# A fourth slot for split weights, norms moved into units, and a new order of work at a gate, in a two-block transformer kernel on one Trainium2 core

## The reference

```python
def _layer(x, ...):                                  # the first block
    h = _rmsnorm(x, ln1_g)
    q, k, v, u = jnp.split(h @ w_in, [...], axis=-1) # 1024, 256, 256, 1024 wide
    q = _rmsnorm(q.reshape(bsz, L, 16, 64), q_norm_g)
    k = _rmsnorm(k.reshape(bsz, L, 4, 64), k_norm_g)
    y_attn = _sliding_window_attention(q, k, v, attn_sinks, rel_bias)   # window 128
    y_ssm = _s5_mixer(u, ..., w_glu)                 # scan over time; y * sigmoid(y @ w_glu)
    mixed = jnp.concatenate([_rmsnorm(y_attn, attn_out_g), _rmsnorm(y_ssm, ssm_out_g)], axis=-1)
    x = x + mixed @ w_out
    h2 = _rmsnorm(x, ln2_g)
    return x + (jax.nn.silu(h2 @ w_ff_gate) * (h2 @ w_ff_up)) @ w_ff_down   # hidden 5632

def second_block(x, ...):                            # two layers
    for layer in range(2):
        hn = rmsnorm(h, norm_mix_pre[layer])
        mix = gmlp_shortconv_mixer(hn, ...) if layer % 2 == 0 else dilated_attention_mixer(hn, ...)
        h = h + rmsnorm(mix, norm_mix_post[layer])
        f = squared_relu_mlp(rmsnorm(h, norm_mlp_pre[layer]), w_up[layer], w_down[layer])  # 8192
        h = h + rmsnorm(f, norm_mlp_post[layer])

def gmlp_shortconv_mixer(h, w_in, w_s, b_s, conv_w, w_out):
    a_u, a_v, g_b, g_c, b_x = jnp.split(h @ w_in, [...], axis=-1)
    a_u, vf = jax.nn.gelu(a_u), jax.nn.gelu(a_v)
    mu = jnp.mean(vf, axis=-1, keepdims=True)
    var = jnp.mean(jnp.square(vf - mu), axis=-1, keepdims=True)
    vn = (vf - mu) * lax.rsqrt(var + LN_EPS)         # v's norm
    mixed = einsum('gts,bnsgc->bntgc', where(causal, w_s, 0), vn) + b_s
    z = g_c * b_x                                    # then a causal convolution of width 3
    return concatenate([a_u * mixed, g_b * y]) @ w_out

def dilated_attention_mixer(h, w_qkv, w_o, positions):
    q, k, v = jnp.split(h @ w_qkv, 3, axis=-1)       # 16 heads of 128, rope on q and k
    ...                                              # three dilations, joined by a softmax
```

## Time and profile before

| | |
|---|---|
| median of 3 runs | 3328.59 us (3328.2 to 3331.68) |
| the profiled execution, its own time | 3326.39 us |
| its span in the trace | 3324.4 us |
| mean granted TensorE clock | 0.989 of full speed |
| busy PE / PEld | 3237.1 us (97%) / 2671.3 (80%) |
| busy DVE / ACT / POOL | 1866.3 us (56%) / 1472.2 (44%) / 80.8 (2%) |
| idle of PE | 3324.4 - 3237.1 = 87.3 us |
| DMA | 593 MB, mean 178 GB/s, 55% of the 16 engines' time |

### The profile page before, as it was taken

How to read it: one execution, slowest core, us unless ns; L and a number is a source line. 1 busy time by engine, 2 the same in 40 slices (tenths; PEclk the granted TensorE clock), 3 DMA queues, 4 the chain that set the end, 5 groups by cost and what they waited for, 6 DMA issues and landing times. The chain is left out here.

```text
span 3324.4 us, 38815 instructions
## 1 busy us (share of the span) xinstructions
PE 3237.1 (97%) x15938; PEld 2671.3 (80%) x15938; DVE 1866.3 (56%) x1978; ACT 1472.2 (44%) x1757; POOL 80.8 (2%) x76
## 2 busy tenths in 40 slices
PE   8989999999999999999999999999999999999998
PEld 6877888888888778878888888878877788888886
DVE  7655655554555545665555555665655655555555
ACT  6534544444444444444444444444444544444443
POOL 1120000000000000000000000000000000000000
PEclk9999999999999999999999999999999999999999
DMA  6334555555555555555555555545455555555554
GB/s 207 113 112 116 177 184 189 191 192 193 193 188 192 179 172 189 192 177 188 189 188 192 189 191 189 189 159 178 151 165 165 176 190 188 189 188 188 187 189 150
DMA packets 185517, 593.19 MB, mean 178 GB/s; under 512 B 12491, under 2 KB 17276, under 8 KB 184828
## 3 DMA queue, kind: packets, MB, share of 16 engines
q1 hardware_dynamic: 185340, 590.70, 54.7%
HBM read 588.54 MB, written 2.12 MB: 178 GB/s over the span
## 5 line engine op out<-in xcount | busy, mean ns | idle before, releaser
L1155 DVE TENSOR_TENSOR LO<-RAW,HI 128x1024 fp32r<-128x1024 f32 (+1 forms) x1104 | 1346.3, 1222 | 1133.4 <-ACT HI L593 1131.2
L593 ACT ACTIVATE HI<-RAW 128x1024 fp32r<-128x1024 f32 (+1 forms) x1104 | 1158.9, 1052 | 1352.4 <-PE PS L2054 1344.0
L2054 PE MATMUL PS<-HI,KPA 128*128 128x512 f32 x5312 | 1476.6, 394 | 13.5 <-ACT HI L593 5.5
L2054 PEld LDWEIGHTS PS<-HI,KPA 128*128 128x128 f32 x5312 | 992.9, 189 | 224.3 <-issue 12.2
L2054 PE MATMUL PS<-HI,KPB 128*128 128x512 f32 x3392 | 935.2, 392 | 4.0 <-DVE ACC L1757 3.4
L2054 PE MATMUL PS<-LO,KPA 128*128 128x512 f32 x2656 | 828.6, 392 | 5.8 <-DVE LO L1155 5.8
L2054 PEld LDWEIGHTS PS<-HI,KPB 128*128 128x128 f32 x3392 | 631.0, 188 | 133.1 <-issue 5.3
L2054 PEld LDWEIGHTS PS<-LO,KPA 128*128 128x128 f32 x2656 | 501.0, 189 | 115.7 <-DVE LO L1155 8.7
L2054 PE MATMUL PS<-LO,KPB 128*128 128x512 f32 x1696 | 524.5, 390 | 0.8 <-DVE KPB L1193 0.8
L2054 PEld LDWEIGHTS PS<-LO,KPB 128*128 128x128 f32 x1696 | 318.6, 188 | 68.8 <-issue 1.2
L622 ACT ACTIVATE KPB<-PS 128x512 fp32r<-128x512 f32 x98 | 58.6, 599 | 181.6 <-PE PS L2114 181.6
(11 more groups left out here) (268 smaller groups left out, 1038.2 us busy)
## 6 DMA issues: line engine op xcount, KB each, us to landing
RAW<-in_w_up SPq DMA_DIRECT2D x128, 1024.0 KB, 5.0
RAW<-in_w_down SPq DMA_DIRECT2D x128, 1024.0 KB, 5.4
RAW<-in_w_qkv SPq DMA_DIRECT2D x48, 1024.0 KB, 5.2
RAW<-in_w_ff_gate SPq DMA_DIRECT2D x88, 512.0 KB, 3.8
RAW<-in_w_ff_up SPq DMA_DIRECT2D x88, 512.0 KB, 4.7
RAW<-in_w_ff_down SPq DMA_DIRECT2D x44, 1024.0 KB, 5.4
RAW<-in_w_in_ab SPq DMA_DIRECT2D x40, 1024.0 KB, 5.0
RAW<-in_w_in SPq DMA_DIRECT2D x16, 1024.0 KB, 5.3
```

The source lines that it names most:

```text
L593: e.activation(HI[:, s % NSPLIT, 0:w], RAW[:, d % NRAW, j, 0:w], ACT.Copy).then_inc(S("hi_made"), 1)
L1155: e.tensor_tensor(LO[:, h, 0:w], RAW[:, d % NRAW, j, 0:w], HI[:, h, 0:w].bitcast(F32), ALU.subtract).then_inc(S("lo_made"), 1)
L2054: ins = e.matmul(PS[:, b + j, 0:cw], l, r[:, h, 512 * j:512 * j + cw], start=(i == 0 and part == 0), stop=(last and part == 2))
```

## The change

It has five parts.

1. **A fourth slot.** From the unit ws0 on there is a slot 3 (HI3, LO3) where the state space's tables (CC) lay, from up1.0 on it is slot 4 (HI4, LO4) where small tables of the first block lay. `make_slots` gives every step the slot that was used longest ago (`plan.slot`, and `plan.was`, the step that used it before); `split_by(i)` says how far HI and LO may be made when step i is at hand. Step s is split once the step `was[s]` is done, so now up to four steps back instead of three.
2. **A split between evacuations.** At the end of the six qkv units named in `SPLIT_BETWEEN` the evacuating engine makes its next HI (ACT) or LO (DVE) after tile 0 and before tile 1.
3. **k's norm goes to the q unit, q's norm is denser, y is fed earlier.** The KD multiplications are in `k_norm`, k's root is taken in the q unit. Both squares of q follow each other on ACT (the second into LG1), there are two roots of 16 columns instead of one of 32, and glu's steps ask for y's chunks by the table `Y_DUE`. k's turns follow glu's steps 1 and 2, q's the steps 5 and 6. ACT makes a sigmoid of one element (WARM) before the gate, and at the gate DVE takes the first two logits between the gate's multiplications.
4. **v's norm goes into ab1.** `v_squares` on ACT, centring, mask and scaling in `mixing` on DVE, and TensorE's mixing starts three steps later.
5. **pre0's turns** in dn1.5.1 are taken between the tiles and after the steps (`first_half`, in `mids` and `sides`), instead of only after them.

```diff
+    def make_slots(self):
+        fourth, moved = self.by_name["ws0"].first, self.by_name["up1.0"].first
+        used = {i: i - NSPLIT for i in range(NSPLIT)}
+        self.slot, self.was, self.taken = [], [], {}
+        for s in range(len(self.steps)):
+            if s == fourth:
+                used[3] = s - 1
+            h = min(used, key=used.get)
+            self.slot.append(4 if h == 3 and s >= moved else h)
+            self.was.append(used[h])
+            used[h] = s
...
+    def split_by(self, i):
+        s = i
+        while s + 1 < len(self.steps) and self.was[s + 1] < i:
+            s += 1
+        return s
...
+Y_DUE = (1, 2, 2, 3, 3, 4, 4, 4)
+SPLIT_BETWEEN = ("qkv0.0", "qkv0.1", "qkv0.2", "qkv1.0", "qkv1.1", "qkv1.2")
+def first_half(feeder):
+    yield
+    for _ in range(4):
+        next(feeder)
+        yield
...
-                if s >= NSPLIT:
-                    q.wait_ge(S("step_done"), s - NSPLIT + 1)
-                e.activation(HI[:, s % NSPLIT, 0:w], RAW[:, d % NRAW, j, 0:w], ACT.Copy).then_inc(S("hi_made"), 1)
+                if plan.was[s] >= 0:
+                    q.wait_ge(S("step_done"), plan.was[s] + 1)
+                if s in plan.taken:
+                    taken(plan.taken[s])
+                e.activation(HI[plan.slot[s]][:, 0:w], RAW[:, d % NRAW, j, 0:w], ACT.Copy).then_inc(S("hi_made"), 1)
...
                 evac(0, u.bank[0])
                 q.wait_ge(S("step_done"), u.last + 1)
+                if name in SPLIT_BETWEEN:
+                    hi(plan.split_by(u.last + 1))
                 evac(1, u.bank[1])
...
             for c in range(4):
                 out_of(2 + c, qT, 2 * c, "qg")
+                if c == 3:
+                    e.activation(WARM[:, 0:1], ONE[:, 0:1], ACT.Sigmoid)
...
-        att = late(attn1(), 4)
-        unit("glu", y_feed(), [S0, S1, q_norm(), att], ahead=1)
+        att = late(attn1(), 1)
+        unit("glu", y_feed(), [S0, S1, q_norm(), att], ahead=Y_DUE)
...
-            q.wait_ge(S("v_centred"), t + 1)
-            q.wait_ge(S("v_squared"), t)
-            e.activation(JK[:, :], AV[:, t, :], ACT.Square, accum_out=vs2[:, t:t + 1]).then_inc(S("v_squared"), 1)
+
+        def v_squares():
+            yield
+            for t in range(2):
+                q.wait_ge(S("v_centred"), t + 1)
+                q.wait_ge(S("v_squared"), t)
+                e.activation(JK[:, :], AV[:, t, :], ACT.Square, accum_out=vs2[:, t:t + 1]).then_inc(S("v_squared"), 1)
+                yield
...
-        unit("ab1", None, (), (), to_sb(lambda t: GC[:, t, :], "pre0"))
+        unit("ab1", None, [v_squares()], (), to_sb(lambda t: GC[:, t, :], "pre0"))
...
         for n in range(2):
             gate_times(n)
+        next(att)
         q.wait_ge(S("gated"), 1)
         next(sf)
         for n in range(2, 4):
             gate_times(n)
-        for _ in range(2):
-            next(att)
+        next(att)
...
-        unit("ab1", None, [late(mxg, 3)])
+        unit("ab1", None, [mxg])
...
-                    pend = [part0()] if i == nu // 2 and c == 0 else []
+                    pend = [first_half(nf0[0])] if i == nu // 2 and c == 0 else []
```

More of the change, by code:

```diff
@@ L23 @@
 NSPLIT = 3
-LA = NSPLIT - 1
 SCRATCH = 1024
@@ L286, in in_units @@
     for i in range(n):
-        while feeder is not None and made < due(i, n, ahead):
+        while feeder is not None and made < (ahead[i] if isinstance(ahead, tuple) else due(i, n, ahead)):
             next(feeder)
@@ L760, in ssm @@
             for k in range(4):
-                for _ in range(3):
+                for _ in range(2 if k == 3 else 3):
                     yield
@@ L980, in scalar @@
                 for c in range(2):
-                    unit(f"dn1.{i}.{c}", None, pend)
+                    unit(f"dn1.{i}.{c}", None, pend, mids=pend if i == nu // 2 else ())
                     for g in pend:
                         drain(g)
-                    pend = [part(nf)] if i == nu // 2 and c == 0 else []
+                    pend = [first_half(nf)] if i == nu // 2 and c == 0 else []
         def dn_added(c, t):
@@ L1667, in vector @@
                 for c in range(2):
-                    unit(f"dn1.{i}.{c}", None, pend, (), add_x(c))
+                    unit(f"dn1.{i}.{c}", None, pend, (), add_x(c), mids=pend if i == nu // 2 else ())
                     added(f"dn1.{i}.{c}")
@@ L2006, in gpsimd, with k_root @@
         S0, S1 = ssm(0), ssm(1)
-        unit("q", [S0, S1])
-        root("k")
+        def k_root():
+            for _ in range(11):
+                yield
+            root("k")
+            yield
+        unit("q", [S0, S1, k_root()])
         def q_root():
-            for _ in range(4):
+            for t in range(2):
+                root(f"q{t}")
                 yield
-            root("q")
-            yield
         unit("glu", [S0, S1, q_root()])
@@ L2028, in matmuls @@
             s = u.first + i
-            h, g = s % NSPLIT, G[u.group]
+            h, g = plan.slot[s], G[u.group]
             kt, ks = chunk(g, i)
@@ L2238, in ssm @@
                 yield
-                for i in range(2):
+                for i in range(2 if k < 3 else 1):
                     if k < 3:
@@ L2363, in tensor @@
         unit("q", None, [pr2, S0, S1])
-        att = late(attn1(), 4)
-        unit("glu", None, [S0, S1, att], ahead=1)
-        for _ in range(2):
-            next(att)
+        att = late(attn1(), 1)
+        unit("glu", None, [S0, S1, att])
+        next(att)
         unit("ws0", None, [s_sums(), att], mids=[att])
@@ L2473, in tensor @@
         mxg = mixing()
-        unit("ab1", None, [late(mxg, 3)])
+        mxl = late(mxg, 6)
+        unit("ab1", None, [mxl])
         unit("ab2")
```

145 lines of the change are left out of this document (91 added, 54 removed).

## The result

The changed kernel took 3317.79 us (median of 9 runs, 3315.93 to 3322.01), the kernel before 3328.59 (9 runs, 3324.01 to 3331.68): ratio 0.997, 95% interval 0.9961 to 0.9979, or 10.8 us less where 17.6 were forecast. TensorE's busy time is the same 3237.1 us; its idle time fell from 87.3 to 78.6.

What follows compares the result with a forecast made beforehand. TensorE, busy nearly throughout, was taken as the bound, so only its waits and clock drops could give time. 9.9 + 2.2 + 1.4 + 10.4 - 6.3 = 17.6 us less: 3308.8 profiled, 3311.0 median; range 3302 to 3320.

Steps and rivals of the forecast that it cites:

- signs of being wrong: Waits over 2 us left in glu, new LO waits in ab1, over 10 us more low clock in qkv, or ends not lengthened.
- Glu: Glu unit: three waits for y's chunks go, 8.14, plus 3.4 of clock, less 1.6 for new waits; gain 9.9 us.
- The gate: At the gate: table load, qT copy and DVE's wait for scores come off, one LO is added; gain 2.2 us.
- The fourth slot: End of ws0: takes 1.4 of a 2.13 us wait through an earlier bias transfer; 0 over the other steps.
- The second block's start: Before the second block and around v's norm: waits of 2.65, 1.87, 1.71 go, plus clock 1.7 and 2.5; gain 10.4 us.
- The splits between: Ends of the qkv units: tile 1's bank comes later, 5.35 us, plus 1.0 for the clock; loss 6.3 us.
- the 1.0 for the clock: Qkv ends: a wait of about 3.7 us may drop the clock, costing 1.7 with six chances in ten.
- A: Rival: waits move from glu to the attention, whose DVE work is unchanged; 3319.5 us, chance 0.17.
- parts 1 to 3: The prediction's terms for glu with the q and k norms, the gate, and the fourth slot; 13.5 us together.
- B: Rival: the qkv ends cost only 0.7 and the slot removes small waits, say 2; 3303.4 us, chance 0.17.
- C: Rival: all six qkv ends wait for a late HI and drop the clock, 3.0 + 3.4 each; 3342.7 us, chance 0.03.
- D: Rival: glu's chunks stay late because of the scan, and v's norm makes splits late inside ab1; 3324 us, chance 0.10.

## Why the prediction was right, and where its sizes were off

The direction held, the sum was 6.8 us too good, and the time lies within the stated range. Of the mechanisms, those of glu's new wait, the gate, pre0's turns and the splits between held; the fourth slot's did not, and in two places the gain came from another part of the change than the one I named (k's multiplications, v's norm). In the traces, where the kernels are 8.7 apart, the misses are 0.4 ahead of glu, 1.3 in it, 0.2 at the gate, 2.4 for the slot, 0.6 up to qkv0.0 and 4.6 at the ends, less 0.6 too little at the second block's start. Two of my own signs of being wrong came true: a wait of over 2 us in glu (2.72, for the scan and not for a chunk), and over 10 us more at 1.2 GHz in the qkv units (13.6 against 3.4). By its own steps:

- *Glu.* 8.6 of 9.9. The allowance for new waits was 1.6, and 2.72 came. The chain was named rightly (the last quarter of the second half, GpSimd and DVE), but I took its durations as unshortened and did not see that they would grow: q's multiplication now lies beside GpSimd's last operation, 1.58 instead of 0.73. The roots of 16 columns took 3.42 and 2.91, against 2.9 (GpSimd, the changed kernel, from 198.95 and 205.45 on). That k's multiplication made the chunk late, which I argued from its 2.55 us, was wrong as a cause: with it gone and the old table the 3.31 became 3.73. What made the chunk late was when it was asked for.
- *The gate.* 2.0 of 2.2 in the trace. Undoing the order alone loses 1.9 in the trace and 1.6 in the times, though of what I had counted (table load, qT copy, DVE's wait) no run undoes one by itself. That the table load is off the path is read from the trace only (ACT, the changed kernel; glu ends at 232.49):

```profile
230.58 1.28 ACT L863 ACT_TABLE_LOAD   x1
231.88 0.20 ACT L863 ACTIVATE WARM<-ONE 128x1 f32<-128x1 f32 x1
231.99 1.04 ACT L646 ACTIVATE HI<-RAW 128x1024 fp32r<-128x1024 f32 x1
232.93 1.55 ACT L959 ACTIVATE GT<-PS 128x512 f32<-128x512 f32 x3
```

  The gate's sigmoid starts 0.44 us after glu's end. The sigmoid of one element starts 0.02 after the load's end, so again no drain is to be seen between the load and what follows.
- *The fourth slot.* Forecast 1.4, measured a loss, 1.0 up to the first FFN unit's second chunk. The wait of 2.33 for the bias rows did go: DVE waits 0.71 there for scores now (285.79). But its next logits wait 1.30 for scores, and DVE comes later to the addition that frees the bank: from TensorE's last turns to that addition pass 1.98 us (290.95 and 292.93), before it was 1.53 (302.16 and 303.69). The wait became 2.58, with 3.4 us at 1.2 GHz in every trace with four slots. In the kernel as changed the slot costs 4.1 us (3.4 by the gains), without the splits between 1.8 by the medians and 4.1 by the gains; only with v's norm in its old place does it take something away, 5.4 us of wait and clock. That it removes nothing over the other steps was right: ACT's HI's wait for TensorE, as in the earlier trace rows. I called three waits the only long ones labelled HI or LO; the trace of before has a longer one at the kernel's start, 2.66 for a LO at 13.80, which the slot, there from ws0 on, cannot reach.
- *The second block's start.* 11.0 against 10.4. pre0's turns: 3.6 by the medians and 4.3 by the trace, of 4.35. v's norm: the sum is right, the attribution is wrong in the main, since the slot alone would have covered all but 1.6 of it; I had given the slot nothing there.
- *The splits between.* This is the term that was mis-sized: 6.3 forecast, 10.6 measured. The waits were well sized: +0.9 at qkv0.2 (1.05 forecast), +1.1 at qkv1.0 (0.9), +3.1 at qkv1.1 (3.0), +0.6 at qkv1.2 (0.4), together 5.7 against 5.35. What failed is the 1.0 for the clock: three more stretches of 3.4 us at 1.2 GHz came, 5.1 us. I gave a drop, with six chances in ten, to one of four lengthened waits.
- *Rivals.* By the number alone the time, 3317.8, lies nearer to A's 3319.5 than to the forecast's 3311. A's mechanism was there in small only: parts 1 to 3 gave 9.6 of 13.5, not 5, since ws0 and ws1 gave back 1.0 instead of gaining 1.4; the larger miss is that of the ends, which A left as forecast. B was wrong on the ends. C's wait of 3.0 was reached at one end only, with 1.7 for the clock instead of 3.4. D's first half (chunks stay late) would have come true had only the other orders moved and not the table.
- *A slip.* The last scores were to come near 243.9; 255.75 less 9.9 and 2.2 is 243.65. They came at 245.60.

The version with three slots, no split between and q's early multiplication took 3303.71 and 3306.07 in two sets, ratios 0.9922 (0.9909 to 0.9936) and 0.9932 (0.992 to 0.9945): faster than both kernels, by 24 to 26 us than the one before beside it and by 12 to 14 than the changed one.

## What to carry to other kernels

Between the two evacuations of a unit nothing should stand unless a third bank pair is free; a split placed there inherits every delay of the engine that feeds it. Two edits that cover the same wait must be priced together, and each undone in both states of the other, or the second one looks worthless. When waits of about two microseconds are lengthened, price the clock at each of them: 3.4 us at 1.2 GHz, 1.7 us lost, came behind most of them here. A wait that looks like a queue's fault may be one of when the work was asked for; change that number alone before moving other work out of the way.
